# Weight tiles woven in pairs and read with a step of two elements

## The chip, the core and the metric

The kernel runs on one core of a Trainium2 chip (trn2). The metric is the time on the device in microseconds (us), the median of the runs shown. TensorE multiplies a stationary operand of 128 x 128 (the weights) with a moving operand of up to 512 columns; each matmul of this kernel comes with a load of its weights, recorded apart as PEld. VectorE (DVE), ScalarE (ACT) and GpSimd (POOL) work beside it, and SyncE (SP) issues most transfers.

## What is computed

Two blocks in a row on 512 tokens with 1,024 features, in float32. The first is run twice (DEPTH = 2), the second has two different layers. Cut to what matters:

```python
for i in range(2):                       # first block
    x = x + 0.5 * rmsnorm(swiglu(rmsnorm(x), w1_gate, w1_up, w1_down))   # 1024 -> 2816 -> 1024
    h = rmsnorm(x) @ w_in
    mixed = concat(stick_breaking(h), latent_attention(h, w_mla_uq, w_mla_ukv), gated_conv(h)) @ w_out
    x = x + rmsnorm(mixed)
    x = x + 0.5 * rmsnorm(swiglu(rmsnorm(x), w2_gate, w2_up, w2_down))
    x = x + rmsnorm(sigmoid(rmsnorm(x) @ w_ple_gate) * (p @ w_ple_proj))
for i in range(2):                       # second block: sparse, then dilated attention, each with a memory
    x = x + mixer_i(rmsnorm(x) @ w_in_i, mem @ w_mem_kv_i) @ w_out_i
    x = x + swiglu(rmsnorm(x), w_gate_up_i, w_down_i)
return rms_norm(x)
```

## The kernel before

**Tiles and pieces.** Activations stand with features on the partitions and tokens along them, so a product of weights and activations is a row of matmuls whose stationary operand is a weight tile of 128 x 128 and whose moving operand is a chunk of up to 512 tokens. On the host `weight_stream` cuts all weights into tiles and packs up to TILES = 8 of them side by side into a piece of 128 x 1,024 float32 (512 KB). SyncE brings the pieces in one after the other, into a ring of four slots (`raw`, lines 546 and on), with some spare slots at the borders of the stages.

**High and low parts.** To keep float32's precision, a weight w is split into WH (rounded to fp32r) and WL = w - WH, and an activation likewise (HH and HL, HIDH and HIDL, TH and TL). Each tile then takes three matmuls: WH x high, WL x high, WH x low, each with its own load of weights. The split of a piece is two operations over its whole width: GpSimd at lines 629 and 631 for the plain pieces, ScalarE and VectorE at lines 1697 and 2240 for the pairs' parts, and at lines 1718 and 2316 for the pieces of the down projection. WL takes the place of raw, WH lies behind it.

**The pair stage.** Of the 22 row blocks of the gate and up projections of a feed-forward, 4 are done plainly and 18 in 9 pairs. A pair is a product of 2 x 2 blocks done with seven block products instead of eight: GpSimd adds parts of the weights (lines 658, 663 and 669, and a transfer that adds, line 651), and `product` (lines 899 to 901) multiplies each sum with 256 tokens, 24 matmuls a product. There are six feed-forwards, so 6 x 9 x 7 products.

**The other users of weight tiles.** `piece` (lines 749 to 751), `chunk_high` and `chunk_low` (757, 758, 761), `half_chunk` (797, 798), the early part of the down projection (982 to 984), `half_piece` (1016 to 1018) and `heads_piece` (1388 to 1390). Nearly all have 512 moving columns. Lines 982 to 984 run over four outputs for each k, the others over the tiles of one output.

**The latent pieces.** In the first block, 8 pieces a layer hold the tiles of w_mla_uq and w_mla_ukv, up to KQ + KKV = 3 + 2 = 5 tiles. GpSimd splits only these five, 640 columns: `rounds(MH, KQ + KKV)`.

**What has a step already.** In the dilated layer, `dil_scores` (line 1250) takes its queries and keys as `PROJ[r, chunk, b::QB]`, every fourth token: 128 elements of 4 bytes with a step of four elements, as stationary and as moving operand, on 64 rows, two such matmuls side by side on the two halves of the rows. Line 1246 does the same with neighbouring tokens. `to_token` (line 1133) transposes blocks of PROJ by a matmul with the identity (in cf); those of the groups 1 and 2 of the dilated layer read `b::QB` too.

**Order.** It is written out by hand, by semaphores between the engines: a piece is loaded when a slot's matmuls are done (`piece_used`, `part_used`), split when landed, and multiplied when split (`w_split`, `part_lo`, `down_lo`).

Of the kernel before, what the change touches and what calls it, by code (L numbers as in the profile page):

```python
# [8 lines left out]
P = 128  # L9
D, S, DEPTH = 1024, 512, 2  # L10
KD = D // P
# [6 lines left out]
KQ, KKV = QR // P, KVR // P  # L18
MH, NOPE, ROPE = 8, 64, 32
# [10 lines left out]
TILES = 8  # L30
# [4 lines left out]
PAIRS = (KF - PLAIN) // 2  # L35
PRODUCTS = 7
HALF = S // 2
HALF_K = KD // 2
EARLY_M = 4
# [3 lines left out]
FFNS = 2 * DEPTH + 2  # L43
# [4 lines left out]
PIECES = DEPTH * LAYER_PIECES + (IN_DSA + 4 + KD + FFN_PIECES) + (IN_DIL + 4 + KD // 2 + FFN_PIECES)  # L48
# [83 lines left out]
def program(nc, A, trips):  # L132
# [3 lines left out]
    at = [-(-nc.sbuf_base // 32) * 32]  # L136
# [7 lines left out]
    def sb(name, shape, dt=F32, offset=None):  # L144
        n = int(np.prod(shape[1:])) * (2 if dt == BF16 else 4)
        o = region(-(-n // 32) * 32) if offset is None else offset
        return nc.alloc_sbuf_tensor_at(name, list(shape), dt, offset=o)
# [5 lines left out]
    HL = sb("HL", [P, KD, S], F32R, offset=HLo)  # L153
# [29 lines left out]
    WH = [sb(f"WH{j}", [P, TILES * P], F32R, offset=o + 4 * KB) for j, o in enumerate(slot_at)]  # L183
# [60 lines left out]
    def sem(name, start=0):  # L244
        credit[name] = start
        return ctx.enter_context(nc.semaphore(name))
# [10 lines left out]
    piece_used = sem("piece_used", AHEAD)  # L257
# [226 lines left out]
    tokens_of = lambda half: slice(half * HALF, (half + 1) * HALF)  # L484
# [27 lines left out]
    sb_exp = lambda i: SBE[i // 2 % 2][:, i % 2, 0:sb_w(SB_UNITS[i][1])]  # L512
    latent_value_bank = lambda c: PD[:, c // 2]

    block = ctx.enter_context(nc.Block())


# [101 lines left out]
    def _(pool):  # L619
# [13 lines left out]
        def ring(pieces, tiles=TILES):  # L633
            nonlocal turn
            for _ in range(pieces):
                split(turn % RING, tiles)
                turn += 1

        def rounds(pieces, tiles=TILES):
            with n.loop(pieces // RING):  # L640
                ring(RING, tiles)

        def border():
            ring(RING)
            pool.wait_ge(hl_ready, n.full(hl_ready, 6))
            n.full(hl_ready, 2)
            split(RING, TILES)
            split(RING + 1, TILES)
# [52 lines left out]
        with n.loop(DEPTH):  # L701
            ffn()
            border()
            rounds(12)
            rounds(MH, KQ + KKV)
            rounds(KD)
            n.full(piece_used, IN_A + MH + KD)
            ffn()
            n.full(piece_used, 2 + KD)
            ring(RING)  # L710
            split(RING, TILES)
            split(RING + 1, TILES)
            n.full(hl_ready, KD)
            ring(RING)
# [20 lines left out]
    def _(pe):  # L735
# [6 lines left out]
            taken += 1  # L742
            return (taken - 1) % RING

        def piece(slot, out, hi, lo, tiles, start=True, stop=True, cols=(0, P), first_tile=0, done=piece_used):

            for t in range(tiles):
                w = slice((first_tile + t) * P + cols[0], (first_tile + t) * P + cols[1])
                pe.matmul(out, WH[slot][:, w], hi[:, t], start=start and t == 0, stop=False)  # L749
                pe.matmul(out, WL[slot][:, w], hi[:, t], start=False, stop=False)  # L750
                mm = pe.matmul(out, WH[slot][:, w], lo[:, t], start=False, stop=stop and t == tiles - 1)  # L751
            if done is not None:
                mm.then_inc(done, 1)

        def chunk_high(slot, out, k, skip=False):
            w = slice(k * P, (k + 1) * P)
            pe.matmul(out, WH[slot][:, w], HH[:, k], start=k == 0, stop=False, skip_group_check=skip)
            pe.matmul(out, WL[slot][:, w], HH[:, k], start=False, stop=False, skip_group_check=skip)

        def chunk_low(slot, out, k, skip=False):  # L760
            mm = pe.matmul(out, WH[slot][:, k * P:(k + 1) * P], HL[:, k], start=False, stop=k == KD - 1, skip_group_check=skip)
            if k == KD - 1:
                mm.then_inc(piece_used, 1)

# [28 lines left out]
            fourth(KD - 1)  # L793

        def half_chunk(slot, out, k, half):
            w, at = slice(k * P, (k + 1) * P), tokens_of(half)
            pe.matmul(out[:, at], WH[slot][:, w], HH[:, k, at], start=k == 0 and half == 0, stop=False, skip_group_check=True)
            pe.matmul(out[:, at], WL[slot][:, w], HH[:, k, at], start=False, stop=False, skip_group_check=True)

# [90 lines left out]
        def product(i, slots, out, start, hi, lo):  # L890

            if i != 6:
                pe.wait_ge(part_lo, n.full(part_lo, 2 if i == 3 else 1))
            slot = slots[i]
            for half in range(2):
                o = out[:, tokens_of(half)]
                for k in range(HALF_K):
                    w = slice((half * HALF_K + k) * P, (half * HALF_K + k + 1) * P)
                    pe.matmul(o, WH[slot][:, w], hi[:, k], start=start and half == 0 and k == 0, stop=False, skip_group_check=True)  # L899
                    pe.matmul(o, WL[slot][:, w], hi[:, k], start=False, stop=False, skip_group_check=True)  # L900
                    mm = pe.matmul(o, WH[slot][:, w], lo[:, k], start=False, stop=half == 1 and k == HALF_K - 1, skip_group_check=True)  # L901
            mm.then_inc(part_used, 1)
# [25 lines left out]
        def ffn(normed=True, first=False, after_heads=False, by_halves=False):  # L928
# [46 lines left out]
            for ks in EARLY_K:  # L975
                pe.wait_ge(down_lo, n.full(down_lo))
                slot = next_slot()
                for j, k in enumerate(ks):
                    pe.wait_ge(hid_ready, hid + k + 1)
                    for m in range(EARLY_M):  # L980
                        w = slice((j * EARLY_M + m) * P, (j * EARLY_M + m + 1) * P)
                        pe.matmul(down_bank(m), WH[slot][:, w], HIDH[:, k], start=k == 0, stop=False)
                        pe.matmul(down_bank(m), WL[slot][:, w], HIDH[:, k], start=False, stop=False)
                        mm = pe.matmul(down_bank(m), WH[slot][:, w], HIDL[:, k], start=False, stop=k == KF - 1)  # L984
                mm.then_inc(piece_used, 1)
            pe.wait_ge(quad_done, n.full(quad_done, 4))
            for m in range(KD):
# [5 lines left out]
                for q, tiles in enumerate(DOWN):  # L993
                    pe.wait_ge(down_lo, n.full(down_lo))
                    if by_halves and m == KD - 1:
                        slot, hi, lo = next_slot(), HIDH[:, 8 * q:], HIDL[:, 8 * q:]
                        mm = half_piece(slot, 0, hi, lo, range(tiles), q == 0, q == 2)
                        if q == 2:
                            mm.then_inc(half_out, 1)
                        mm = half_piece(slot, 1, hi, lo, range(tiles), q == 0, q == 2, q == 2)  # L1000
# [6 lines left out]
        def half_piece(slot, half, hi, lo, order, start=True, stop=True, mean_square=False, late={}):  # L1007

            out, tokens = LAST[half], tokens_of(half)
            for i, t in enumerate(order):  # L1010
                if t in late:
                    pe.wait_ge(ol_ready, n.now(ol_ready) - late[t])
                if mean_square and i == len(order) - 4:
                    mean_square_of_first_half()
                w = slice(t * P, (t + 1) * P)
                pe.matmul(out, WH[slot][:, w], hi[:, t, tokens], start=start and i == 0, stop=False)
                pe.matmul(out, WL[slot][:, w], hi[:, t, tokens], start=False, stop=False)
                mm = pe.matmul(out, WH[slot][:, w], lo[:, t, tokens], start=False, stop=stop and i == len(order) - 1)
            return mm
# [361 lines left out]
        def heads_piece(which, slot, out, first_tile=0, done=piece_used):  # L1381

            order, late = OUT_ORDER[which]
            for i, t in enumerate(order):
                if t in late:
                    pe.wait_ge(ol_ready, n.now(ol_ready) - late[t])
                w = slice((first_tile + t) * P, (first_tile + t + 1) * P)
                pe.matmul(out, WH[slot][:, w], OH[which][:, t], start=i == 0, stop=False)
                pe.matmul(out, WL[slot][:, w], OH[which][:, t], start=False, stop=False)
                mm = pe.matmul(out, WH[slot][:, w], OL[which][:, t], start=False, stop=t == order[-1])  # L1390
            mm.then_inc(done, 1)
# [1450 lines left out]
def weight_stream(a):  # L2842
    out = np.zeros((PIECES, P, TILES, P), np.float32)
    pairs = np.zeros((FFNS, PAIRS, 4, P, TILES, P), np.float32)
    at = ffns = 0
# [28 lines left out]
    for l in range(DEPTH):  # L2874
        ffn(a["w1_gate"][l], a["w1_up"][l], a["w1_down"][l])
        w = a["w_in"][l]
# [25 lines left out]
    cols = np.concatenate([np.arange(h * HD, (h + 1) * HD) for h in order])  # L2902
    w = a["l0_w_in_2"]
# [25 lines left out]
    gu = a["l1_w_gate_up_2"]  # L2929
    ffn(gu[:, :FF], gu[:, FF:], a["l1_w_down_2"])  # L2930
    assert at == PIECES, (at, PIECES)
    return out.reshape(PIECES, P, TILES * P), pairs.reshape(FFNS * PAIRS * 4, P, TILES * P)


def vectors(a, inv):
# [41 lines left out]
```

## Time and profile before

| what | value |
|---|---|
| median of 2 runs | 3,335.03 us (3,332.34 to 3,337.73) |
| the profiled execution's span | 3,337.3 us |
| instructions | 51,827 |
| mean granted clock of TensorE | 0.993 |
| read from HBM | 355.84 MB, 108 GB/s over the span |

TensorE's clock is granted at its full 2.4 GHz in nearly all of the span. A row of the groups names the line, the engine, the operation, the tiles written and read (the output first), their shapes, the count, the busy time, the mean time of one instruction, and the idle time before them. A matmul's record is longer than the time from one start to the next, as neighbours overlap; the starts in the timeline tell the rate.

### The profile page before, as it was taken

The page shows a single profiled execution, that of the slowest core. Times are in us where ns is not written, and L with a number is a line of the kernel's source. Part 1 is how long each engine was busy: PE and PEld are TensorE (multiplying, and loading weights), DVE is VectorE, ACT ScalarE, POOL GpSimd, SP SyncE. Part 2 cuts the span into 40 slices and gives each one's busy share as a digit, 9 for nine tenths or more (in the row PEclk, how much of TensorE's full clock was granted, in tenths as well). Part 3 has the DMA queues.
Part 4 walks back from the last instruction along what each step waited for, and adds up shares of the span by engine and source line. Part 5 has one row for each costly group of instructions (what it writes and reads, how often), then busy time and mean ns, then how long its engine had stood idle before and what let it go on. Part 6 is the DMA issues. An engine that isn't in the chain of part 4 may idle for free.

```text
span 3337.3 us, 51827 instructions
## 1 busy us (share of the span) xinstructions
PE 3229.6 (97%) x19480; PEld 2729.8 (82%) x19487; DVE 2059.6 (62%) x2673; ACT 1359.2 (41%) x2335; POOL 1345.4 (40%) x643
## 2 busy tenths in 40 slices
PE   8999999999999999999999999998999999999998
PEld 7998775789877899877579987765789987879986
DVE  7774444586647876354477765678477734477753
ACT  5553225344435445322444543324435521254542
POOL 6320562554116541065164404656553107635300
PEclk9999999999999999999999999999999999999999
DMA  4543221255332454322035533221145433215532
GB/s 156 159 143 104 90 87 32 70 152 151 114 123 83 138 160 120 105 83 87 19 99 153 153 117 108 101 68 34 51 135 166 123 103 108 82 57 146 168 104 95
DMA packets 99977, 362.59 MB, mean 109 GB/s; under 512 B 11088, under 2 KB 11344, under 8 KB 99536
## 3 DMA queue, kind: packets, MB, share of 16 engines
q1 hardware_dynamic: 88704, 320.90, 29.4%
q0 software_dynamic: 7776, 28.32, 5.1%
q10 hardware_dynamic: 3312, 10.86, 0.9%
q8 instruction: 122, 2.00, 0.2%
q14 instruction: 63, 0.52, 0.0%
HBM read 355.84 MB, written 4.19 MB: 108 GB/s over the span
## 4 chain that ended last, share of the span: by engine, by line
PE 73%; DVE 10%; issue 6%; ACT 4%; POOL 3%; DMA 3%; DVEq 0%; ACTq 0%; POOLq 0%; SPq 0%
PE psC L749 4%; PE psC L751 4%; PE psC L750 4%; PE psA L749 4%; PE psA L751 4%; PE psA L750 4%; PE psD L899 2%; PE psD L900 2%; PE psD L901 2%; PE psB L899 2%; PE psB L900 2%; PE psB L901 2%; DVE WL L2240 2%; DMA Y<-in_ws 2%; PE psB L984 2%
## 5 line engine op out<-in xcount | busy, mean ns | idle before, releaser
L629 POOL TENSOR_TENSOR WH<-raw,scalars 128x1024 fp32r<-128x1024 f32 (+1 forms) x194 | 377.8, 1948 | 1206.5 <-DMA raw<-in_w 1143.3
L2240 DVE TENSOR_TENSOR WL<-raw,WH 128x1024 fp32r<-128x1024 f32 x324 | 447.9, 1385 | 70.5 <-POOL raw L663 39.8
L631 POOL TENSOR_TENSOR WL<-raw,WH 128x1024 fp32r<-128x1024 f32 (+1 forms) x194 | 471.2, 2429 | 15.2
L1697 ACT ACTIVATE WH<-raw 128x1024 fp32r<-128x1024 f32 x324 | 340.4, 1053 | 48.9 <-DMA raw<-in_ws 37.2
L2316 DVE TENSOR_TENSOR WL<-raw,WH 128x1024 fp32r<-128x1024 f32 (+1 forms) x144 | 163.1, 1135 | 307.4 <-ACT WH L1718 305.8
L658 POOL TENSOR_TENSOR raw<-raw,Y 128x1024 f32<-128x1024 f32 x54 | 133.4, 2471 | 509.6 <-DMA raw<-in_ws 509.6
L1718 ACT ACTIVATE WH<-raw 128x1024 fp32r<-128x1024 f32 (+1 forms) x144 | 141.9, 989 | 375.7 <-DMA raw<-in_w 375.7
L749 PE MATMUL psA<-HH,WH 128*128 128x512 f32 x560 | 230.0, 411 | 0.0
L751 PE MATMUL psA<-HL,WH 128*128 128x512 f32 x560 | 218.5, 390 | 0.0
L750 PE MATMUL psA<-HH,WL 128*128 128x512 f32 x560 | 218.3, 390 | 0.0
L899 PE MATMUL psD<-TH,WH 128*128 128x256 f32 x720 | 202.0, 281 | 6.2 <-DVE psC L2287 2.7
L900 PE MATMUL psD<-TH,WL 128*128 128x256 f32 x720 | 200.5, 279 | 0.0
L901 PE MATMUL psD<-TL,WH 128*128 128x256 f32 x720 | 200.3, 278 | 0.0
L749 PE MATMUL psC<-HIDH,WH 128*128 128x512 f32 x484 | 191.8, 396 | 3.5 <-DVE WL L2316 3.5
L750 PE MATMUL psC<-HIDH,WL 128*128 128x512 f32 x484 | 191.4, 396 | 0.0
L751 PE MATMUL psC<-HIDL,WH 128*128 128x512 f32 x484 | 191.4, 395 | 0.0
L899 PE MATMUL psB<-TH,WH 128*128 128x256 f32 x576 | 161.9, 281 | 5.1 <-ACT psB L1734 5.1
L669 POOL TENSOR_TENSOR raw<-raw,raw 128x1024 f32<-128x1024 f32 x54 | 142.8, 2645 | 47.3 <-PE psB L901 27.5
L900 PE MATMUL psB<-TH,WL 128*128 128x256 f32 x576 | 160.6, 279 | 0.0
L901 PE MATMUL psB<-TL,WH 128*128 128x256 f32 x576 | 160.4, 278 | 0.0
L899 PEld LDWEIGHTS psD<-TH,WH 128*128 128x128 f32 x720 | 135.9, 189 | 8.3 <-DVE psC L2287 3.5
L663 POOL TENSOR_TENSOR raw<-raw,raw 128x1024 f32<-128x1024 f32 x54 | 134.0, 2482 | 13.4 <-POOL raw L658 11.6
(540 smaller groups left out, 9631.1 us busy)
## 6 DMA issues: line engine op xcount, KB each, us to landing
raw<-in_w SPq DMA_DIRECT2D x338, 512.0 KB, 3.5
raw<-in_ws SPq DMA_DIRECT2D x216, 512.0 KB, 3.6
Y<-in_ws SPq DMA_DIRECT2D x54, 512.0 KB, 4.7
raw<-in_ws POOLq DMA_DIRECT2D x54, 512.0 KB, 5.4
X<-in_x ACTq DMA_DIRECT2D x4, 512.0 KB, 9.5
NRAW<-in_mem ACTq DMA_DIRECT2D x2, 1024.0 KB, 7.2
out<-Y SPq DMA_DIRECT2D x8, 256.0 KB, 2.1
POSI<-in_pos ACTq DMA_DIRECT2D x4, 256.0 KB, 2.6
```

Source lines behind the costliest of these rows:

```text
L629: pool.tensor_tensor(WH[j][:, 0:w], raw[j][:, 0:w], zero[:, 0:1].broadcast_to([P, w]), ALU.subtract).then_inc(w_hi, 1)
L631: pool.tensor_tensor(WL[j][:, 0:w], raw[j][:, 0:w], WH[j][:, 0:w], ALU.subtract).then_inc(w_split, 1)
L669: pool.tensor_tensor(raw[slots[5]][:], raw[slots[2]][:], raw[slots[3]][:], ALU.add).then_inc(sum_ready, 1)
L749: pe.matmul(out, WH[slot][:, w], hi[:, t], start=start and t == 0, stop=False)
L750: pe.matmul(out, WL[slot][:, w], hi[:, t], start=False, stop=False)
L751: mm = pe.matmul(out, WH[slot][:, w], lo[:, t], start=False, stop=stop and t == tiles - 1)
L899: pe.matmul(o, WH[slot][:, w], hi[:, k], start=start and half == 0 and k == 0, stop=False, skip_group_check=True)
L900: pe.matmul(o, WL[slot][:, w], hi[:, k], start=False, stop=False, skip_group_check=True)
L901: mm = pe.matmul(o, WH[slot][:, w], lo[:, k], start=False, stop=half == 1 and k == HALF_K - 1, skip_group_check=True)
L1697: act.activation(WH[slots[i]][:], DX if i == 6 else raw[slots[i]][:], ACT.Copy).then_inc(part_hi, 1)
L2240: dve.tensor_tensor(WL[slots[i]][:], DX if i == 6 else raw[slots[i]][:], WH[slots[i]][:], ALU.subtract).then_inc(part_lo, 1)
L2316: dve.tensor_tensor(WL[j][:, 0:w], raw[j][:, 0:w], WH[j][:, 0:w], ALU.subtract).then_inc(down_lo, 1)
```

## The change

The pieces are woven on the host: tiles 0 and 1 of a piece alternate column by column (column 0 of tile 0, column 0 of tile 1, column 1 of tile 0, ...), likewise tiles 2 and 3, and so on. The bytes of a piece stay in the same place as a whole, and no buffer moves. Each read of a weight tile by TensorE takes 128 columns with a step of two elements out of the 256 columns of its pair. Since the fifth tile of a latent piece has its columns among those of the empty sixth, the latent pieces are split over six tiles. An unused argument of `piece` goes.

```diff
+    woven = lambda t: slice(t // 2 * 2 * P + t % 2, (t // 2 + 1) * 2 * P, 2)
...
-            rounds(MH, KQ + KKV)
+            rounds(MH, KQ + KKV + 1)
...
-        def piece(slot, out, hi, lo, tiles, start=True, stop=True, cols=(0, P), first_tile=0, done=piece_used):
+        def piece(slot, out, hi, lo, tiles, start=True, stop=True, first_tile=0, done=piece_used):
...
-                w = slice((first_tile + t) * P + cols[0], (first_tile + t) * P + cols[1])
+                w = woven(first_tile + t)
...
         def chunk_high(slot, out, k, skip=False):
-            w = slice(k * P, (k + 1) * P)
+            w = woven(k)
...
-            mm = pe.matmul(out, WH[slot][:, k * P:(k + 1) * P], HL[:, k], start=False, stop=k == KD - 1, skip_group_check=skip)
+            mm = pe.matmul(out, WH[slot][:, woven(k)], HL[:, k], start=False, stop=k == KD - 1, skip_group_check=skip)
...
-                    w = slice((half * HALF_K + k) * P, (half * HALF_K + k + 1) * P)
+                    w = woven(half * HALF_K + k)
...
-                        w = slice((j * EARLY_M + m) * P, (j * EARLY_M + m + 1) * P)
+                        w = woven(j * EARLY_M + m)
...
-    return out.reshape(PIECES, P, TILES * P), pairs.reshape(FFNS * PAIRS * 4, P, TILES * P)
+    weave = lambda w: np.ascontiguousarray(w.reshape(-1, P, TILES // 2, 2, P).swapaxes(3, 4)).reshape(-1, P, TILES * P)
+    return weave(out), weave(pairs)
```

`half_chunk`, `half_piece` and `heads_piece` are changed in the same way.

## Rows read from the trace of the kernel before

**Rows 1.** The page: busy shares of the engines, and the chain that ended last

```profile
PE 3229.6 (97%) x19480; PEld 2729.8 (82%) x19487; DVE 2059.6 (62%) x2673; ACT 1359.2 (41%) x2335; POOL 1345.4 (40%) x643
...
PE 73%; DVE 10%; issue 6%; ACT 4%; POOL 3%; DMA 3%; DVEq 0%; ACTq 0%; POOLq 0%; SPq 0%
```

**Rows 2.** Whole span, busy time and count by engine: tile WH, tile WL, line 899

```profile
0.00:3338.00 3338.00, 2692.61 (x11280) 1902.09 (x11280) 676.60 (x522) 533.54 (x522) 846.91 (x388) 0.99 0.36 109
...
0.00:3338.00 3338.00, 1853.38 (x5648) 1067.84 (x5648) 676.60 (x522) 471.18 (x194) 0.99 0.36 109
...
0.00:3338.00 3338.00, 851.29 (x3024) 573.18 (x3024) 0.99 0.36 109
```

**Rows 3.** Timeline of TensorE, pair stage: start us, us, engine, line, tiles, shape

```profile
59.80 0.28 PE L899 MATMUL psC<-HH,WH 128*128 128x256 f32 x1
...
61.84 0.28 PE L901 MATMUL psC<-HL,WH 128*128 128x256 f32 x1
...
100.18 0.28 PE L901 MATMUL psB<-TL,WH 128*128 128x256 f32 x1
...
102.23 0.28 PE L901 MATMUL psB<-TL,WH 128*128 128x256 f32 x1
```

**Rows 4.** Timeline of TensorE, 512 moving columns, on HIDH and on HH

```profile
304.83 0.40 PE L750 MATMUL psC<-HIDH,WL 128*128 128x512 f32 x1
...
306.47 0.39 PE L751 MATMUL psC<-HIDL,WH 128*128 128x512 f32 x1
...
466.02 0.39 PE L751 MATMUL psA<-HL,WH 128*128 128x512 f32 x1
...
471.01 0.39 PE L749 MATMUL psA<-HH,WH 128*128 128x512 f32 x1
```

**Rows 5.** The largest group of weight loads of the pair stage, on TH

```profile
L899 PEld LDWEIGHTS psD<-TH,WH 128*128 128x128 f32 x720 | 135.9, 189 | 8.3 <-DVE psC L2287 3.5 <-issue 2.8 <-DVE WL L2240 1.0
```

**Rows 6.** Loads of lines 1250 (step of four) and 1246: min/median/max ns

```profile
L1250 PEld LDWEIGHTS psA<-PROJ x32: 304/326/329, 2897.2 to 2912.5; 64*128 64x128 f32 x32
...
L1246 PEld LDWEIGHTS psA<-PROJ x16: 182/184/187, 2896.9 to 2911.6; 64*128 64x128 f32 x16
```

**Rows 7.** Timeline of loads, neighbours merged: lines 1246 and 1250

```profile
2901.39 0.30 PEld L1246 LDWEIGHTS psA<-PROJ 64*128 64x128 f32 x4 [0.17 <-ACT PR L1856]
2901.71 1.01 PEld L1250 LDWEIGHTS psA<-PROJ 64*128 64x128 f32 x8
```

**Rows 8.** Loads of transposes, line 1133, without a step and with one

```profile
L1133 PEld LDWEIGHTS psC<-cf,PROJ x8: 140/141/143, 2903.3 to 2906.2; 128*128 128x128 f32 x8
...
L1133 PEld LDWEIGHTS psC<-cf,PROJ x16: 195/210/213, 2908.2 to 2916.3; 128*128 128x128 f32 x16
...
2905.89 0.47 PEld L1133 LDWEIGHTS psC<-cf,PROJ 128*128 128x128 f32 x4
...
2908.21 0.56 PEld L1133 LDWEIGHTS psC<-cf,PROJ 128*128 128x128 f32 x4
```

**Rows 9.** GpSimd's splits: groups by shape

```profile
L631 POOL TENSOR_TENSOR WL<-raw,WH 128x1024 fp32r<-128x1024 f32 x178 | 445.7, 2504 | 14.0
L629 POOL TENSOR_TENSOR WH<-raw,scalars 128x1024 fp32r<-128x1024 f32 x178 | 357.7, 2009 | 1163.1 <-DMA raw<-in_w 1099.9 <-DVE HL L2064 63.2
...
L631 POOL TENSOR_TENSOR WL<-raw,WH 128x640 fp32r<-128x640 f32 x16 | 25.5, 1596 | 1.3
L629 POOL TENSOR_TENSOR WH<-raw,scalars 128x640 fp32r<-128x640 f32 x16 | 20.2, 1260 | 43.4 <-DMA raw<-in_w 43.4
```

**Rows 10.** Waits of TensorE for GpSimd's splits: us in total, times, longest

```profile
PE psA L757 <- POOL WL L631: 9.9, 1, 9.9
...
PE psC L757 <- POOL WL L631: 2.2, 2, 1.2
```

**Rows 11.** Timeline of TensorE, bf16 weights, 256 moving columns

```profile
2902.95 0.28 PE L1253 MATMUL psA<-mb,identb 128*128 128x256 bf16 x1
...
2903.28 0.27 PE L1255 MATMUL psA<-mb,identb 128*128 128x256 bf16 x1
```

More of the change, by code:

```diff
@@ L795, in half_chunk @@
         def half_chunk(slot, out, k, half):
-            w, at = slice(k * P, (k + 1) * P), tokens_of(half)
+            w, at = woven(k), tokens_of(half)
             pe.matmul(out[:, at], WH[slot][:, w], HH[:, k, at], start=k == 0 and half == 0, stop=False, skip_group_check=True)
@@ L1014, in half_piece @@
                     mean_square_of_first_half()
-                w = slice(t * P, (t + 1) * P)
+                w = woven(t)
                 pe.matmul(out, WH[slot][:, w], hi[:, t, tokens], start=start and i == 0, stop=False)
@@ L1386, in heads_piece @@
                     pe.wait_ge(ol_ready, n.now(ol_ready) - late[t])
-                w = slice((first_tile + t) * P, (first_tile + t + 1) * P)
+                w = woven(first_tile + t)
                 pe.matmul(out, WH[slot][:, w], OH[which][:, t], start=i == 0, stop=False)
```

## The prediction

> **What bounds the kernel now.** I read the shares of the page first, then the chain that ended last, then the groups of TensorE's instructions. TensorE is busy for 97% of the span, and the chain that ended last runs through it for 73% [rows 1]. Of its 19,480 matmuls 11,280 have a tile of WH as their weights and 5,648 a tile of WL [rows 2]; together these are 16,928, and every one of them is touched by the change, since each loads its weights with an instruction of its own. So the kernel is bound by the rate at which pairs of one weight load and one matmul go through TensorE, and the question is whether that rate changes.
>
> The timeline gives the rate by shape. With 256 moving columns (the seven products of a pair, lines 899 to 901, 3 x 3,024 = 9,072 matmuls [rows 2]), from the start at 100.18 us to that at 102.23 us there are 18 steps on TH and TL, 0.114 us each, and from 59.80 to 61.84 us 17 steps on HH and HL, 0.120 us each [rows 3]. Three of a pair's seven products take HH and four take TH, so the mean is near (3 x 0.120 + 4 x 0.114) / 7 = 0.117 us. The other 16,928 - 9,072 = 7,856 are mostly 512 columns wide: 0.227 us each on HH (22 steps from 466.02 to 471.01), 0.234 us on HIDH (7 steps from 304.83 to 306.47) [rows 4], about 0.230 on the whole.
>
> What hides a weight load? A load starts as the matmul before its own one starts, and is recorded with 189 ns [rows 5]. That is longer than the 117 ns of a slot, so the record holds a latency that is pipelined. The rate of a load is to be had where the matmul is short: the transposes of line 1133 have 128 moving columns, and four loads take 0.47 us, of which the last is 0.14: (0.47 - 0.14) / 3 = 0.110 us from load to load [rows 8]. Two pairs of loads of line 1246, each pair side by side on half the rows, take 0.30 us, of which 0.18 is the last: 0.11 to 0.12 [rows 7]. So a load without a step occupies its path for about 0.11 us. In the 512-wide slots it has 0.12 us to spare. In the 256-wide slots it has 0.004 to 0.010 us. **That small margin, 9,072 times, is where the change can cost.**
>
> **The change part by part.**
>
> (a) DMA, VectorE, ScalarE and the split on GpSimd read and write the same bytes at the same addresses without a step; the order of columns means nothing to a copy, a subtraction or a sum, and both halves of each sum (lines 658 to 669) are woven alike. The sizes of the transfers stay. Cost: nothing, and nothing covers it.
>
> (b) The split of the 16 latent pieces widens from 640 to 768 columns, since tile 4 now lies in the columns 512 to 767. Between the two widths that the trace shows, 384 columns cost 2,009 - 1,260 = 749 ns for the high and 2,504 - 1,596 = 908 ns for the low part [rows 9]; 128 columns are 0.25 and 0.30 us, so 0.55 us a piece and 16 x 0.55 = 8.8 us of GpSimd. Before these pieces GpSimd sits idle until the landing, 43.4 us over the 16, 2.7 us each [rows 9]. A piece gets ready 0.55 us later; the only matmuls of the whole trace that waited for a split of GpSimd are those of line 757, which take no latent piece [rows 10]. Cost: nothing; without that cover at most 8.8 us.
>
> (c) The 16,928 weight loads read 128 elements of 4 bytes with 8 bytes between them. The trace has no step of two, but a step of four: line 1250 reads PROJ[..., b::QB] as weights and as moving operand, and the later transposes of line 1133 read b::QB as the one operand that is not the identity; without a step stand line 1246 and the earlier transposes. Their loads take 326 ns (median; 304 at the least) against 184 without a step [rows 6]; in the transposes 210 against 141 [rows 8]. From load to load it is (1.01 - 0.33) / 3 = 0.227 us against the 0.11 [rows 7], and in the transposes (0.56 - 0.21) / 3 = 0.117 against 0.110 [rows 8]. In line 1250 the moving operand has the step too and may hold the slot up; but its loads are 304 ns long even at the least, so the load itself is slow. The bounds for a step of two are 0.11 us (nothing added) and 0.23 us (as bad as a step of four).
>
> Which end? At a step of four the added time is 326 - 184 = 142 ns for 128 elements, 1.1 ns for an element, and the rate of the load is about halved. A reader that fetches 16 bytes at a time and needs two elements out of each fetch explains this: without a step it gets four and has more than it needs, with four it gets one and runs at half rate, with two it gets exactly two. A reader that fetches 8 bytes explains the same rows: two elements without a step, one at a step of four, and one at a step of two. The rows alone can't tell these apart. I take the first, because in the transposes, where the load is the shorter kind (141 ns), full use of one fetch per element added 7 ns to the slot: a path that is slowed to just its limit loses little. By it a load of two elements per fetch stays near 0.11 us, at the most 0.12.
>
> The Trainium skill (SBUF — State Buffer, "SBUF cachelines") says that lines have 16 bytes and that two hits on a line are enough for full bandwidth; by it the step of two is free and the step of four isn't. That the step of four is slow agrees with the rows (326 against 184 ns); that two is free no run here shows. The same section says that each access to another line pays a penalty; read without its threshold of two hits that is case C below. By the page's threshold the sum would be the 3,337 us of the profile, by the row of the step of four some 4,430 us.
>
> Sum: (a) 0, (b) 0, (c) if the load stays below 0.114 us, 0. Should it reach 0.120, the 9,072 x 4 / 7 = 5,184 matmuls on TH and TL lose up to 0.006 us, 31 us, and if the 512-wide slots on HH (about half of 7,856) went from 0.227 to 0.233 as well, 24 us more. I take a small part, 5 us. Against the profile's 3,337.3 us that is 3,342; the median of the two runs is 3,335.0, 2.3 us less, so 3,340 us.
>
> **The rivals.**
>
> *Case A, a step of two is free or nearly so.* 3,325 to 3,395 us (0 to 55 us more, and the spread of the runs). For it: the arithmetic above, and the 512-wide slots with half their time free. Against it: only an inference carries it.
>
> *Case B, a step of two reads like a step of four.* The load then takes 0.227 us and bounds each 256-wide slot: 9,072 x (0.227 - 0.117) = 998 us; with 0.233 us (an extra 6 ns, as between TH and HH) 9,072 x 0.116 = 1,052 us; the 512-wide slots lose some 7,856 x 0.003 = 24 us. The time is 3,337 + 1,022 to 3,337 + 1,076, about 4,360 to 4,415 us, or some 4,430 if about a hundred first loads after a wait add their 0.12 us each. For it: the rows fit a fetch of 8 bytes just as well. It decides as soon as a load passes 0.117 us by more than a few ns, since the products have no more room.
>
> *Case C, each new line costs, with no threshold.* The load goes from 0.110 (one line in four elements) to 0.227 (one in each), so at one in two it is 0.110 + 0.117 x (0.25 / 0.75) = 0.149 us, and the products lose 9,072 x (0.149 - 0.117) = 290 us: 3,627 us. Against it: the transposes lose only 7 ns where all lines are new.
>
> *Case D, faster.* The slots stand above those of bf16 weights: from 2,902.95 to 2,903.28 us three steps of 256 columns take 0.11 us each [rows 11]. The excess depends on the moving buffer (0.114 on TH, 0.120 on HH), as if reads of weights and of moving data got in each other's way. If the new rhythm removed it all, 9,072 x 0.007 + 7,856 x 0.014 = 174 us would go: 3,163 us. It decides if the excess is a collision of addresses and not a fixed cost. Nothing in the rows says that more lines collide less.
>
> **How the numbers follow.** Case A 0.77, B 0.13, C 0.06, D 0.04. The likeliest is A, 3,340 us, with its own range of 3,325 to 3,395. To hold 8 in 10 the range takes in the milder half of C (some 0.03) and reaches from 3,315 to 3,500. A is within 2%, which is about what a measurement of this kernel can tell from no change; B and C are slower by more; D is faster by more. One in a hundred of A may come out above 2%. So faster 0.04, same 0.76, slower 0.20.
>
> **What would show it.** In the trace after, the loads of line 899 (189 ns now) tell the cases apart: up to 197 ns in A, near 230 in C, over 300 in B. The starts of matmuls on TH stay at 0.114 us in A (0.120 at its upper end), 0.149 in C, 0.227 in B. The 512-wide slots stay at 0.227 and 0.233 in A and C. GpSimd's groups of 640 columns become 768 columns wide, with about 1.51 and 1.90 us. I would be wrong above all if the reader of weights fetches less than 16 bytes at a time.

## The result and the profile after

The changed kernel took 3,362.05 us (median of 2 runs, 3,359.52 to 3,364.57) against 3,335.03 us before: 1.0078 times as long, with a 95% interval of 1.0059 to 1.0097. That is 27 us more, and clear of noise, though less than 2%. The kernel before was run 32 times more beside the experiments, with medians of 3,336.0 and 3,336.5 us. The profiled execution of after has a span of 3,358.3 us, 21.0 more than that of before.

The page of after, the span, the busy shares and the chain that ended last:

```profile
span 3358.3 us, 51827 instructions
...
PE 3257.9 (97%) x19480; PEld 2798.6 (83%) x19487; DVE 2058.4 (61%) x2673; ACT 1360.3 (41%) x2335; POOL 1352.0 (40%) x643
...
PE 79%; DVE 9%; issue 5%; ACT 4%; DMA 2%; POOL 1%; DVEq 0%; ACTq 0%; POOLq 0%; SPq 0%
```

Beside [rows 1] TensorE's matmuls are busy for 28.3 us more and its weight loads, which lie beside them, for 69; no other engine for more than 7. In the two views of waits TensorE's own add up to 96.7 us before and 89.5 after, 7.2 less; 28.3 - 7.2 = 21.1 is the change of the span. So the time went into TensorE's slots (the slot of a matmul is the time from its start to the next one's), and a quarter of it was won back in shorter waits.

Weight loads and matmuls of after by group (line, engine, operation, tiles, shapes, count, busy us, mean ns of one, idle before):

```profile
L901 PEld LDWEIGHTS psD<-TH,WH 128*128 128x128 f32 x720 | 140.0, 194 | 6.4 <-DVE psC L2289 3.3 <-issue 2.2 <-DVE WL L2242 0.9
...
L752 PEld LDWEIGHTS psA<-HH,WL 128*128 128x128 f32 x560 | 108.4, 194 | 25.8 <-issue 5.1
...
L902 PE MATMUL psD<-TH,WL 128*128 128x256 f32 x720 | 203.6, 283 | 0.0
...
L752 PE MATMUL psA<-HH,WL 128*128 128x512 f32 x560 | 220.7, 394 | 0.0
...
L752 PE MATMUL psC<-HIDH,WL 128*128 128x512 f32 x484 | 189.8, 392 | 0.0
```

A load's record grew from 189 ns [rows 5] to 194, no more. The matmuls' records did not all go one way (before: 279, 390 and 396 ns): those on TH got 4 ns longer, those on HH 4 ns longer, and those on HIDH 4 ns *shorter*. The same three groups in the trace of before:

```profile
L900 PE MATMUL psD<-TH,WL 128*128 128x256 f32 x720 | 200.5, 279 | 0.0
...
L750 PE MATMUL psA<-HH,WL 128*128 128x512 f32 x560 | 218.3, 390 | 0.0
...
L750 PE MATMUL psC<-HIDH,WL 128*128 128x512 f32 x484 | 191.4, 396 | 0.0
```

The timeline of TensorE in the same stages, beside [rows 3] and [rows 4]:

```profile
100.92 0.28 PE L901 MATMUL psB<-TH,WH 128*128 128x256 f32 x1
...
103.68 0.28 PE L903 MATMUL psB<-TL,WH 128*128 128x256 f32 x1
...
305.50 0.39 PE L751 MATMUL psC<-HIDH,WH 128*128 128x512 f32 x1
...
307.35 0.39 PE L753 MATMUL psC<-HIDL,WH 128*128 128x512 f32 x1
...
467.87 0.39 PE L752 MATMUL psA<-HH,WL 128*128 128x512 f32 x1
...
469.50 0.40 PE L753 MATMUL psA<-HL,WH 128*128 128x512 f32 x1
```

On TH 23 steps in 2.76 us are 0.120 us each (0.114 before), on HIDH 8 steps in 1.85 us are 0.231 (0.234 before), on HH 7 steps in 1.63 us are 0.233 (0.227 before). Averaged over all matmuls of a kind in the trace, from the start of the matmul before each to its own (gaps over 0.4 us left out), in ns:

| moving operand, columns | matmuls | before | after | difference x count |
|---|---|---|---|---|
| TH, TL, 256 | 5,167 | 116.3 | 120.5 | +21.7 us |
| HH, HL, 256 | 4,030 | 120.6 | 121.0 | +1.6 us |
| HH, HL, 512 | 3,536 | 226.9 | 232.4 | +19.4 us |
| HIDH, HIDL, 512 | 3,032 | 233.2 | 229.9 | -10.0 us |
| HIDH, HIDL, 256 | 264 | 115.2 | 121.6 | +1.7 us |

These come to 34 us, some 6 more than the 28.3 us of busy time. The two are not the same measure, as some of the gaps hold short waits; the difference was not taken apart further.

GpSimd's wider split is there as forecast, and the waits of TensorE for GpSimd's splits are the old ones [rows 10]:

```profile
L633 POOL TENSOR_TENSOR WL<-raw,WH 128x768 fp32r<-128x768 f32 x16 | 30.4, 1902 | 1.3
L631 POOL TENSOR_TENSOR WH<-raw,scalars 128x768 fp32r<-128x768 f32 x16 | 24.0, 1500 | 36.3 <-DMA raw<-in_w 36.3
...
PE psA L759 <- POOL WL L633: 10.2, 1, 10.2
...
PE psC L759 <- POOL WL L633: 2.1, 2, 1.0
```

Its work on these pieces grew by 8.7 us, and its idle time before them fell from 43.4 us [rows 9] to 36.3: 7.1 of the 8.7 us lie in it.

### The profile page after: what moved, and what is told of

Read it like the earlier page. It is cut to its first block, busy times and chain, and to the rows that moved or that the text cites. A ratio compares the mean times of both kernels' runs of the same rounds, so it can differ in the third digit from the quotient of the medians.

```text
span 3358.3 us, 51827 instructions
## 1 busy us (share of the span) xinstructions
PE 3257.9 (97%) x19480; PEld 2798.6 (83%) x19487; DVE 2058.4 (61%) x2673; ACT 1360.3 (41%) x2335; POOL 1352.0 (40%) x643
## 4 chain that ended last, share of the span: by engine, by line
PE 79%; DVE 9%; issue 5%; ACT 4%; DMA 2%; POOL 1%; DVEq 0%; ACTq 0%; POOLq 0%; SPq 0%
PE psA L751 4%; PE psC L751 4%; PE psC L752 4%; PE psC L753 4%; PE psA L753 4%; PE psA L752 4%; PE psD L901 3%; PE psD L902 3%; PE psD L903 3%; PE psB L901 2%; PE psB L902 2%; PE psB L903 2%; PE psC L902 2%; PE psC L901 2%; PE psC L903 2%
## 5 line engine op out<-in xcount | busy, mean ns | idle before, releaser
L671 POOL TENSOR_TENSOR raw<-raw,raw 128x1024 f32<-128x1024 f32 x54 | 141.4, 2618 | 61.3 <-PE psB L903 32.9
L903 PEld LDWEIGHTS psD<-TL,WH 128*128 128x128 f32 x720 | 140.4, 195 | 0.0
```

## The experiments

**Theory.** A load reads its 128 elements from 16-byte lines. A step of two doubles the lines, and the time of a load rises from at most 0.113 us to 0.120, which bounds the products. Beside it, the reads of weights and of the moving operand disturb each other by an amount that depends on the distance of their addresses, and a step of two sets this to one middling value everywhere. **Rivals:** a price for each new line without a threshold (case C of the prediction), a stall that is not the load's own time, and differences between the buffers that come from other engines or transfers.

### e1_grid: TensorE alone, steps and distances

The kernel holds only blocks of 24 matmuls, each a line of its own, for example:

```python
for a in seq(2, HH + 64, 256): mm = pe.matmul(*a[0], start=a[1], stop=a[2])   # step, moving operand's place, columns
```

> Not the reference's computation: only TensorE works, on float32r data, in blocks of 24 matmuls, one source line a block, with weights and moving operand placed as in the kernel before. The first part has 64 or 128 moving columns, so that the load sets the rate, with a step of 1, 2, 3, 4 and 8 elements; the rest has 256 and 512 columns with steps of 1, 2 and 4 and the moving operand at different distances from the weights. Theory (a load takes two passes over 128 elements and needs two elements out of each 16 bytes for its full rate): from start to start about 110 ns at step 1, 110 to 120 at step 2, more at step 3 (between), about 230 at steps 4 and 8; with 256 columns step 2 gives 113 to 120 ns and step 4 about 230. Rival C (a price for each new 16 bytes without a threshold): 110, 149, 188, 227, 227. Rival (the 6 ns that the step added on TH are a stall of the moving operand and not the load's own time): step 2 stays at 110 where the load sets the rate. For 512 columns the theory of collisions by address expects the slot at step 1 to be 227 at some distances and 233 at others, with nothing but TensorE at work, and step 2 to turn 227 into 233 and 233 into 230; if the difference between HH and HIDH came from other engines or transfers, all distances give one value here.

The timeline of TensorE (start, time of the whole block; 64 and 128 columns in turn; lines 61 and 62 have step 1, 65 and 66 step 3, 67 and 68 step 4, 69 and 70 step 8), and two stretches of it in the view of windows (the 1.00 and the 0.50 before the last two numbers are the granted clock):

```profile
67.90 2.76 PE L61 MATMUL psA<-big 128*128 128x64 f32 x24
70.50 4.40 PE L62 MATMUL psA<-big 128*128 128x128 f32 x24
...
84.94 5.27 PE L65 MATMUL psA<-big 128*128 128x64 f32 x24
90.02 5.36 PE L66 MATMUL psA<-big 128*128 128x128 f32 x24
95.18 5.73 PE L67 MATMUL psA<-big 128*128 128x64 f32 x24
100.72 5.84 PE L68 MATMUL psA<-big 128*128 128x128 f32 x24
106.35 5.88 PE L69 MATMUL psA<-big 128*128 128x64 f32 x24
...
68.00:70.00 2.00, 2.00 (x21) 2.00 (x19) 0.00 (x0) 0.00 (x0) 0.00 (x0) 1.00 0.03 8
86.00:112.00 26.00, 26.00 (x116) 26.00 (x116) 0.00 (x0) 0.00 (x0) 0.00 (x0) 0.50 0.00 1
```

This first part missed its aim for all steps but one: from about 71.6 us on, in the second narrow block, the clock was granted at 0.50, 1.2 GHz, so what follows can't be held against the numbers expected. Step 1 still had the full clock. In the block of 64 columns (line 61) the first two starts are 0.03 us apart, and the other 23 steps to the start of line 62 take (2.60 - 0.03) / 23 = 0.112 us each: this is the rate of a load without a step where nothing else sets the slot. The load of a step of two was never measured in this way at the full clock.

The part at half clock tells something else. From block to block, at step 3, (90.02 - 84.94) / 24 = 0.212 us; at step 2 it was the same. 256 cycles of 1.2 GHz are 0.213 us, so at this clock a load takes two cycles for each of its 128 columns. The same count at 2.4 GHz would be 0.107 us, 5 ns less than line 61 shows. At step 4 it is (100.72 - 95.18) / 24 = 0.231 us, at half the clock, and the second part of the same kernel gives 0.233 at the full clock: what limits a step of four does not follow TensorE's clock.

The second part, at the full clock, gave for 256 columns 0.120 us at step 2 and 0.233 at step 4, wherever the moving operand lay (0.118 to 0.122, and 0.233 to 0.236). With 512 columns and step 1 it was 0.228 where the moving operand was 0, 256, 512 or 1,024 bytes or 16 KB from its first place, 0.229 at 64, 0.232 at 128, 0.233 at 32 bytes and in the arena's place. There is no other engine and no transfer here, so such a difference as that between HH and HIDH comes from addresses alone. That it is the distance, and not the moving operand's own place, is shown by lines 167 and 169, where the weights were moved into the arena too, so that the distance is 0 again: 0.120 us with 256 columns and 0.228 with 512. One expectation was met at one place of four: at step 2, 512 columns at a distance of 192 gave 0.230 us with both operands 16 KB further on (line 162), but 0.233 in lines 129, 141 and 147, as much as at step 1.

### e5_classes: steps at the full clock, and distances

> Not the reference's computation: only TensorE works, in blocks of 24 matmuls, one source line a block. First 256 and 384 moving columns with steps of 1, 2, 3, 4, 5 and 8 at the full clock (in the first grid the narrow blocks had fallen to half clock), then the distance between moving operand and weights in 16-byte steps from 0 to 256 with 256 and 512 columns and steps of 1 and 2, then blocks at the distances 0, 64, 128 and 192 twice in a row. Theory (the rate of the load depends on the 16-byte lines it touches): 256 columns: 120 ns at step 1 and 2 for distance 0, about 175 at step 3 (96 lines a pass against 128), 233 at step 4, 5 and 8. Rival (full or half rate and nothing between): step 3 at 120 or at 233. Theory of the distance: only the distance modulo 256 bytes counts, the value at 256 is that at 0; at step 1 with 256 columns it is 120 at distance 0 and 113 to 119 elsewhere, with 512 columns 227 at 0 and 229 to 234 elsewhere; at step 2 it is 118 to 122 and 230 to 234 everywhere, nearly independent of the distance. Rival (the order of blocks before decides, not the distance): the repeated blocks differ from the first ones by as much as distances do.

The timeline of TensorE; 256 columns, distance 0 modulo 256 bytes, steps 1, 2, 3, 4, 5 and 8 in the lines 62 to 67, and 384 columns from line 68:

```profile
67.22 3.04 PE L62 MATMUL psA<-big 128*128 128x256 f32 x24
70.09 3.04 PE L63 MATMUL psA<-big 128*128 128x256 f32 x24
72.97 4.39 PE L64 MATMUL psA<-big 128*128 128x256 f32 x24
77.19 5.76 PE L65 MATMUL psA<-big 128*128 128x256 f32 x24
82.79 5.62 PE L66 MATMUL psA<-big 128*128 128x256 f32 x24
88.25 5.95 PE L67 MATMUL psA<-big 128*128 128x256 f32 x24
94.04 4.35 PE L68 MATMUL psB<-big 128*128 128x384 f32 x24
```

From each start to the next, over 24:

| step | 16-byte lines in 128 elements | us a slot | us / (2 x lines) |
|---|---|---|---|
| 1 | 32 | 0.120 | (not bound by lines) |
| 2 | 64 | 0.120 | 0.00094 |
| 3 | 96 | 0.176 | 0.00092 |
| 4 | 128 | 0.233 | 0.00091 |
| 5 | 128 | 0.228 | 0.00089 |
| 8 | 128 | 0.241 | 0.00094 |

The theory expected 0.175 at step 3, the rival that knows only full and half rate 0.120 or 0.233. At steps 3 to 8 the slot is 1.8 to 1.9 ns for each line that the load touches (the table writes it as two reads of 0.89 to 0.94 ns; that each line is read twice is only a guess from the two cycles a column of e1). Steps 4, 5 and 8 touch as many lines and still differ, from 0.228 to 0.241 us, so lines are most of the price and not all of it. By the price of steps 3 and 4 a step of 2 would need 64 x 1.82 = 117 ns, just above the 112 of a load without a step. That is an estimate; what is measured is that the slot at step 2 is 0.118 to 0.122 us over all distances below, so the load itself takes no more than 0.118. Case C, which would have step 2 at 0.149, is out.

Is it the load's own time that grew, or a stall of the matmul? The loads of lines 68 and 69 (384 columns, steps 1 and 2) speak for the first: they are recorded with 189 and 194 ns in the mean, so the record of a load is 5 ns longer at step 2 also here, where the slot did not grow (0.175 and 0.173 us). It is no proof, since with 512 columns, where a load has more than 0.1 us to spare, step 2 moves the slot as well (below). No run tells the two apart.

Now the distance. Lines 107 and 108 have distance 0, 512 columns, step 1 and 2; 177 (step 1) and 179 (step 2) distance 192 and 256 columns; 193 (step 1) and 195 (step 2) distance 192 and 512 columns. Line 97 is step 1 at distance 192 with 256 columns in the sweep, 141 has the same operands as 195:

```profile
215.27 5.63 PE L107 MATMUL psB<-big 128*128 128x512 f32 x24
220.74 5.76 PE L108 MATMUL psB<-big 128*128 128x512 f32 x24
226.34 5.72 PE L109 MATMUL psB<-big 128*128 128x512 f32 x24
...
186.67 2.99 PE L97 MATMUL psA<-big 128*128 128x256 f32 x24
189.50 3.04 PE L98 MATMUL psA<-big 128*128 128x256 f32 x24
...
404.95 5.76 PE L141 MATMUL psB<-big 128*128 128x512 f32 x24
410.55 5.76 PE L142 MATMUL psB<-big 128*128 128x512 f32 x24
...
540.52 2.89 PE L177 MATMUL psA<-big 128*128 128x256 f32 x24
543.25 2.88 PE L178 MATMUL psA<-big 128*128 128x256 f32 x24
545.97 3.05 PE L179 MATMUL psA<-big 128*128 128x256 f32 x24
548.86 3.04 PE L180 MATMUL psA<-big 128*128 128x256 f32 x24
...
618.28 5.76 PE L193 MATMUL psB<-big 128*128 128x512 f32 x24
623.88 5.76 PE L194 MATMUL psB<-big 128*128 128x512 f32 x24
629.49 5.69 PE L195 MATMUL psB<-big 128*128 128x512 f32 x24
635.01 5.68 PE L196 MATMUL psB<-big 128*128 128x512 f32 x24
```

| distance | 256 columns, step 1 | step 2 | 512 columns, step 1 | step 2 |
|---|---|---|---|---|
| 0 | 0.120 | 0.120 | 0.228 | 0.233 |
| 192 | 0.114 | 0.120 | 0.233 | 0.230 |

These four pairs are the kernel's: before, the products on HH have distance 0 to their weights, three of the four products on TH have 192 and one (the fifth product of a pair, weights in slot 8, in the same arena) has 0; HH in the plain pieces has 0, HIDH in the down projection 192. Over all sixteen distances of the sweep, step 1 gave 0.115 to 0.120 us with 256 columns and 0.228 to 0.236 with 512, step 2 0.118 to 0.122 and 0.230 to 0.234. The distance 256 gave the values of 0 within 1 ns.

The rival on the order of blocks is partly right. A block repeated at once agreed with the first within 0.2 ns of a slot in most cases and 1 ns at the most. But at distance 192 with 256 columns and step 1 the sweep gave (189.50 - 186.67) / 24 = 0.118 us and line 177, at another place, 0.114; in the kernel it is 0.1134. And line 141, with the very operands of line 195, gave (410.55 - 404.95) / 24 = 0.233 us, not 0.230. So the distance isn't all; what ran before a block counts for 3 ns there, and it or the place for 4 ns with 256 columns. The table's 0.230 is one of two values that the same operands can have; which of them the kernel has is known from the kernel alone (229.9 ns on HIDH).

### e2_pairs_only and e3_pieces_only: the change in two halves

```diff
-    return weave(out), weave(pairs)
+    return out.reshape(PIECES, P, TILES * P), weave(pairs)      # e2: w = woven(...) in product alone
...
+    return weave(out), pairs.reshape(FFNS * PAIRS * 4, P, TILES * P)   # e3: woven(...) in all but product
```

> Only the parts of the pairs are woven and read with a step of two, the plain pieces stay as before. By the slots of the two traces (5,184 matmuls on TH and TL from about 115.8 to 120.5 ns, those on HH unchanged) this part alone costs 20 to 26 us: 3,355 to 3,361 us, a ratio of 1.006 to 1.008. Rival (the whole cost is in the 512-wide slots on HH, and the pairs' stage is bound by its preparation): 0 to 5 us.

> Only the plain pieces (and those of the down projection) are woven, the pairs' parts stay as before. About 3,300 slots on HH go from 227 to 233 ns (+18 to 20 us) and about 3,700 on HIDH, CH and OHa from 233.3 to 230 (-12 us): 5 to 10 us in all, 3,340 to 3,345 us, ratio 1.001 to 1.003. With e2 it should add up to the 27 us of the whole change. Rival (all slots lose alike): over 20 us.

e2 took 3,355.19 us, 1.0063 times as long as before (1.0049 to 1.0077), e3 3,343.38 us, 1.0028 times (1.0017 to 1.0038). As parts of 3,336 us these are 21 and 9 us, and together 30 (5 either way for e2, 3.5 for e3), where the whole change has 26 (20 to 32), so they add up within the noise. Each rival is out by its interval. In e3's trace the matmuls of HIDH have 230.0 ns from start to start and those on HH with 512 columns 232.4, as in after, with TH at 115.7, near the 116.3 of before; in e2's it is the other way round (233.2, 226.9 and 120.6). Neither half moves the slots of the other.

### e4_step_of_four: the other side of the threshold

```diff
-    woven = lambda t: slice(t // 2 * 2 * P + t % 2, (t // 2 + 1) * 2 * P, 2)
+    woven = lambda t: slice(t // 4 * 4 * P + t % 4, (t // 4 + 1) * 4 * P, 4)
```

> Four tiles are woven instead of two, read with a step of four elements (16 bytes); the latent pieces are split over eight tiles and the down projection's pieces over eight as well. Theory: one element in each 16 bytes, the load takes about 0.23 us, the products of the pairs go from 0.117 to about 0.23 us (9,072 x 0.116 = 1,050 us) and the 512-wide slots from 0.230 to 0.235 or 0.24 (40 to 80 us): 4,400 to 4,480 us. Rival (the load's rate is set by something else than the bytes between elements, so four costs little more than two): under 3,450 us.

It took 4,468.51 us, 1.3401 times as long (1.3371 to 1.3431). Its groups of loads and of matmuls on TH:

```profile
L902 PEld LDWEIGHTS psD<-TH,WL 128*128 128x128 f32 x720 | 237.4, 330 | 0.0
...
L902 PE MATMUL psD<-TH,WL 128*128 128x256 f32 x720 | 285.3, 396 | 0.0
```

The load has 330 ns, near line 1250's 326 before [rows 6], the products come every 233.5 ns, the 512-wide matmuls on HH every 234 and those on HIDH every 239. From four elements a line to two costs 26 us, from two to one 1,106 us more. Case B, which gave this price to the step of two, had 4,360 to 4,415 us, at most some 4,430. It missed by some 40 us, about half of it in the 512-wide matmuls, which lost 7 ns on HH and 5 on HIDH where it had 3.

### e6_arena_64 and e7_arena_64_woven: 64 bytes

```diff
-    ar = region(88 * KB)
+    ar = region(88 * KB + 64) + 64
```

> The kernel before, step of one, with everything in the 88 KB arena (HID, HIDH, HIDL, TH, TL, CH, OHa and the slots 4 to 8) 64 bytes further on, so that its distance to the weights in the slots 0 to 3 and 10 goes from 192 to 0 modulo 256 bytes. Theory of the distance: the 512-wide slots on HIDH, CH and OHa go from 233 to 227 ns (about 3,500 x 6.4 = 22 us less), and the products on TH whose weights lie in the slots 2, 3 and 10 (three of seven, 3,888 matmuls) from 113.4 to 119.5 or 120 (about 24 us more): 3,330 to 3,345 us, ratio 0.998 to 1.003, but both slots moved. Rival (other engines or the buffer as such make the difference): no slot moves.

> The changed kernel with the arena 64 bytes further on. By the first grid a step of two at distance 0 takes 233.3 ns with 512 columns, where HIDH now has 230.0: about 3,500 x 3.3 = 12 us more than the changed kernel, 3,370 to 3,378 us, ratio 1.010 to 1.013; the products stay at 120. Rival (at a step of two the distance plays no part): as the changed kernel, 3,362 us, ratio 1.008.

e6, in the kernel before, took 3,337.86 us, 1.0004 times as long (0.9995 to 1.0013): nothing, as two shifts cancel. From start to start, HIDH with 512 columns went from 233.2 to 226.7 ns and TH from 116.3 to 120.4. A group of each:

```profile
L900 PE MATMUL psD<-TH,WL 128*128 128x256 f32 x720 | 203.7, 283 | 0.0
...
L750 PE MATMUL psC<-HIDH,WL 128*128 128x512 f32 x484 | 188.3, 389 | 0.0
```

e7, in the changed kernel, took 3,376.15 us, 1.0118 times as long (1.0103 to 1.0134), 14 us more than the changed kernel; HIDH went from 229.9 to 235.2 ns, and the products stayed at 120. The blocks alone had given 233.3; the 2 ns on top are not explained. At step two the distance counts a little less on HIDH (5.3 ns against 6.5 at step one), but it does count.

### e8_hid_64: 64 bytes where they help

```diff
-    HID = sb("HID", [P, KF, S], offset=ar)
+    HID = sb("HID", [P, KF, S], offset=ar + 64)      # HIDL too, and HIDH at ar + KF * 2 * KB + 64
```

> The kernel before, step of one, with only HID, HIDL and HIDH 64 bytes further on: the distance to the weights in the slots 0 to 3 is 0 for the down projection, and that of TH and TL stays 192. Theory of the distance: 3,036 slots of 512 columns go from 233.3 to 226.9 ns, 19 us less, nothing else moves: 3,313 to 3,319 us, ratio 0.993 to 0.996. Rival (the down projection is bound by its transfers or splits, not by TensorE): ratio 1.000.

It took 3,320.86 us, 0.9947 times as long as before (0.9933 to 0.9960), 18 us less by this ratio and 16 by the medians, with no instruction changed. The ratio is the one expected; the time is 2 us above its range, as the kernel before stood at 3,336.5 us in this series. One slot moved that was to stay: 264 matmuls on HIDH with 256 columns went from 115 to 121 ns, 1.7 us. TensorE's busy time is 3,210.4 us against 3,229.6 before [rows 1]: 19.2 us less, where 3,032 x (233.2 - 226.7) = 19.7 was to be had. This kernel is faster than both, by less than 1% and clear of noise. Its group on HIDH, and its busy shares:

```profile
L983 PE MATMUL psA<-HIDH,WL 128*128 128x512 f32 x264 | 102.7, 389 | 0.0
...
PE 3210.4 (97%) x19480; PEld 2732.6 (82%) x19487; DVE 2056.8 (62%) x2673; ACT 1359.8 (41%) x2335; POOL 1343.4 (40%) x643
```

## Why the prediction was right, and where it was not

**What bounds the kernel** held: the whole of the change lies in the slots of TensorE.

**(a) and (b)** held. The copies, sums and transfers are as long as before, and the wider split had 1.50 and 1.90 us for the 1.51 and 1.90 forecast, 7.1 of the 8.7 us in time that GpSimd spends waiting for its pieces, and the matmuls that waited for a split of GpSimd are the old ones, of line 759.

**(c), the choice between the two ends,** held. The slot stays at 0.120 us, as a reader of 16 bytes needs, and e5 fits it: by the price of steps 3 and 4, 1.82 ns a line, two elements a line come to 117 ns, where the load takes 112 anyway (e1, line 61). The argument from the transposes, that a path slowed to just its limit loses little, pointed the right way. If a transpose reads each line once, which no run shows, half that price makes 128 x 0.91 = 117 ns, and [rows 8] gave 0.117 us. The Trainium skill (SBUF — State Buffer, its note on SBUF "cachelines") has lines of 16 bytes and full bandwidth from two hits a line. The slots of e5 agree with 16 bytes (step 3 at 0.176 us, steps 4, 5 and 8 within 0.228 to 0.241) and nearly with the two hits: 0.120 us is 6% above the 0.113 of the best case at step one. Below two hits the loss is gradual, 0.176 us at step 3.

**The size** was wrong. The two terms that could be lost were worked out as 31 and 24 us, and then "I take a small part, 5 us". That choice is the step that failed: most of both came in, 21.7 + 1.6 us in the pairs and 19.4 us on HH with 512 columns. For the pairs the text had the means to see it: on TH it had found a margin of 4 ns, and the transposes had shown a loss of 7. For the 512-wide slots on HH it had none, since the load has 0.12 us to spare there; e1 and e5 show that these 6 ns come from the step and the distance between the operands, and not from the load's rate. For the same reason the sign that "the 512-wide slots stay at 0.227 and 0.233" failed: they went to 0.232 and 0.230. Against these stood a term that the sum lacked, the 10 us that HIDH gained, and 7 us of shorter waits; what was left is 27 us between the medians and 21 between the two profiled executions. So the range of case A (3,325 to 3,395) held the time, and the point in it, 3,340, was 22 us too low; that it was not further off owes something to luck, as neither the gain on HIDH nor the shorter waits were forecast. The text also took 2% for what a measurement can tell; the interval here is 0.2% either way, and the loss is clear of it.

**The split of the pair stage** was also wrong in its reason. "Three of a pair's seven products take HH and four take TH" was read as a difference of the buffers, 0.120 against 0.114 us. In the trace of before the matmuls of the one product on TH whose weights are in slot 8 take 119 ns, and e5 and e6 show that it is mainly the distance between weights and moving operand modulo 256 bytes. So 3,888 matmuls and not 5,184 had 0.006 us to lose, and the mean slot on TH was 116 ns and not 114.

**Case B** is what a step of four does, nearly (e4). **Case C** fell with e5. **Case D** had the right suspicion, that the excess over the shortest slot is a matter of addresses, but not that a new rhythm would lift it: at step two the slot goes up on TH and on HH with 512 columns, where it was low, and down on HIDH, where it was high. The gain is to be had at step one, by 64 bytes (e8).

**Open.** Why the slot depends on the distance, and why the distance 0 is among the worst for 256 columns and the best for 512, no run shows. Nor is it explained why the same distance can give 0.113 and 0.118 us, or the same operands 0.230 and 0.233. Whether the 7 ns that a step of two adds on TH are the load's own time or a stall of the matmul is open. At most 6 of them are the load's, as the slot at step two is 0.118 us at some distances and a load without a step takes 0.112; the rest wants the narrow blocks of e1 at the full clock.

## What to carry to other kernels

A weight load has a rate of its own, and where it is close to the matmul's slot (here 0.112 and 0.114 us) every small price on it counts as often as there are matmuls; find the slot by the starts in the timeline, not by the records, and count a price larger than the margin in full. Keep float32 weights at two elements or more in 16 bytes: two cost this kernel 0.8%, one costs 34%. When matmuls of one shape have different slots on different buffers, work out the distances between weights and moving operand modulo 256 bytes and try a shift of the one buffer whose matmuls gain: in e8 64 bytes, which took 512-wide matmuls from 192 to 0, were worth 0.5% with the same instructions. In e6 the same shift took 256-wide matmuls along, which lost as much, and nothing was left.

## What the runs showed of the hardware

- Loads of 128 x 128 float32r weights without a step came every 0.112 us at 2.4 GHz (e1, line 61) and every 0.213 us at 1.2 GHz, two cycles a column. With a step of 3 to 8 elements the slot was 1.8 to 1.9 ns for each 16-byte line touched (e5), and at step four it was the same at both clocks (0.231 and 0.233 us).
- With nothing but TensorE at work, the slot of a load and a matmul without a step depends on the distance of the two operands modulo 256 bytes: 0.113 to 0.120 us with 256 columns, 0.227 to 0.236 with 512. What ran before moves it by some ns too (0.230 or 0.233 us for the same operands at a step of two).
- In e1 the granted clock fell to 0.50, the level of 1.2 GHz, at about 71.6 us, in narrow blocks of 64 and 128 columns; TensorE had no idle time before that (2.00 of 2.00 us from 68 to 70 us) nor at the low level (26.00 of 26.00 us).
